# Placing: POOL makes the second one-hots of three batches in four

## The reference, cut to what matters

```python
q = (x @ w_q).reshape(N, PEER_HEADS, 2, PEER_D_HALF)
s = jnp.einsum('nhpd,pkd->nhpk', q, sub_keys)            # 8 heads, 2 halves, 128 keys each
s_top, i_top = lax.top_k(s, PEER_TOPK)                   # 16 of each half
cand = (s_top[:, :, 0, :, None] + s_top[:, :, 1, None, :]).reshape(N, PEER_HEADS, 256)
best, best_pos = lax.top_k(cand, PEER_TOPK)              # 16 pairs
expert = idx1 * N_KEYS + idx2                            # one of 128 x 128 experts
g = softmax(best)
act = gelu(einsum('cd,ced->ce', x_c, u[e_c]))            # 128 experts per token
out = einsum('ce,ced->cd', g_c * act, v[e_c])
```

## Time and profile before

| | |
|---|---|
| runs | 3749.11 us median (3741.89 to 3754.56, 3 runs) |
| profiled execution | 3739.43 us, span 3737.3 us |
| mean granted clock of TensorE | 0.927 |
| busy share of the span | PE 84%, DVE 71%, ACT 28%, POOL 53% |
| placing | from about 1565 to 1787.5 us, its loop about 216 us |

### The profile page before, as it was taken

One profiled execution on the slowest core, in us unless ns is written; L12 is line 12 of the kernel. 1 busy time (PEld: TensorE's weight loads), 2 busy tenths in 40 slices (PEclk: granted clock), 3 DMA queues, 4 the chain that ended last, 5 costly groups with the idle time before them and its releaser, 6 DMA issues. The chain is left out here.

```text
span 3737.3 us, 47455 instructions
## 1 busy us (share of the span) xinstructions
PE 3150.9 (84%) x15281; PEld 2082.0 (56%) x15281; DVE 2641.1 (71%) x5953; ACT 1045.5 (28%) x1817; POOL 1983.8 (53%) x1776
## 2 busy tenths in 40 slices
PE   5687699789859989377477899998999999999995
PEld 4446244556424333266355667676666666766663
DVE  2226788698475687999677778787777787886446
ACT  4441044366111000276311222222222222222112
POOL 0001565454245887222367677776777677776443
PEclk9888899899979999688788999999999999999997
DMA  6523577766577997258899999999999999999996
GB/s 244 201 85 120 170 265 248 215 214 215 221 251 284 314 339 246 102 172 245 315 379 374 353 408 408 404 405 382 409 399 408 381 405 404 408 405 378 366 345 240
DMA packets 411751, 1133.01 MB, mean 303 GB/s; under 512 B 34088, under 2 KB 129576, under 8 KB 411488
## 3 DMA queue, kind: packets, MB, share of 16 engines
q0 software_dynamic: 221184, 805.40, 57.7%
q1 hardware_dynamic: 174544, 317.82, 23.5%
q10 hardware_dynamic: 15888, 8.13, 0.7%
HBM read 1077.51 MB, written 53.71 MB: 303 GB/s over the span
## 5 line engine op out<-in xcount | busy, mean ns | idle before, releaser
L2272 POOL DMA_INDIRECT exp_value_row<-in_v_rows,exp_v_id x568 | 715.2, 1259 | 278.2 <-issue 176.1
L2319 DVE CUSTOM_DVE_ANT_0 edge_row<-edge_row,edge_x 128x1024 f32<-128x1024 f32 x480 | 583.6, 1218 | 289.0 <-DMA edge_row<-in_u_rows,edge_u_id 255.0
L2264 POOL DMA_INDIRECT edge_row<-in_u_rows,edge_u_id x480 | 508.2, 1059 | 329.2 <-DVE edge_dot L2319 178.3
L376 POOL DMA_INDIRECT ahead_row<-in_u_rows,keep_expert_id x256 | 336.3, 1314 | 347.8 <-DVE keep_dot L386 284.6
L2153 PE MATMUL exp_a_ps<-exp_xT_hi,exp_u_hi 128*128 128x512 f32 x1024 | 409.7, 400 | 19.1 <-DVE exp_u_lo L2288 10.0
L2168 PE MATMUL exp_o_ps<-exp_v_hi,exp_w_hi 128*128 128x512 f32 x1024 | 339.1, 413 | 80.5 <-DVE keep_acc L2383 80.3
L2153 PE MATMUL exp_a_ps<-exp_xT_lo,exp_u_hi 128*128 128x512 f32 x1024 | 401.5, 392 | 0.0
L2153 PE MATMUL exp_a_ps<-exp_xT_hi,exp_u_lo 128*128 128x512 f32 x1024 | 401.1, 392 | 0.0
L2383 DVE TENSOR_TENSOR keep_acc<-exp_o_ps,keep_acc 128x1024 f32<-128x1024 f32 x256 | 311.5, 1219 | 115.9 <-PE exp_o_ps L2168 114.6
L386 DVE CUSTOM_DVE_ANT_0 ahead_row<-ahead_row,ahead_x 128x1024 f32<-128x1024 f32 x256 | 304.0, 1220 | 76.6 <-DMA ahead_row<-in_u_rows,keep_expert_id 72.9
L2139 PE MATMUL exp_v_ps<-exp_value_row,exp_hot 128*32 128x512 f32 x2272 | 278.6, 602 | 60.5 <-DMA exp_value_row<-in_v_rows,exp_v_id 60.1
(11 more groups left out here) (380 smaller groups left out, 5134.3 us busy)
## 6 DMA issues: line engine op xcount, KB each, us to landing
edge_u_raw<-in_uT SPq DMA_DIRECT2D x130, 512.0 KB, 6.7
exp_v_raw<-in_v_rows SPq DMA_DIRECT2D x128, 512.0 KB, 6.7
exp_g_raw<-scratch_g SPq DMA_DIRECT2D x128, 256.0 KB, 8.3
scratch_g<-place_grid SPq DMA_DIRECT2D x3, 8192.0 KB, 36.2
proj_ctx_mod_slab<-in_w_mod SPq DMA_DIRECT2D x8, 2048.0 KB, 14.4
cheads_room<-in_w_in SPq DMA_DIRECT2D x10, 1024.0 KB, 5.1
heads_early_room<-in_w_in SPq DMA_DIRECT2D x10, 1024.0 KB, 9.7
exp_value_row<-in_v_rows,exp_v_id POOLq DMA_INDIRECT x568, 7.7
```

Of the source, the lines that this page charges most:

```text
L376: nc.gpsimd.indirect_dma_start(out=ahead.row[:, n % KEY_RING, :], out_offset=None, in_=io["u_rows"], in_offset=bass.IndirectOffsetOnAxis(a ...
L2264: nc.gpsimd.indirect_dma_start(out=key_row[:, j % RING, :], out_offset=None, in_=io["u_rows"], in_offset=bass.IndirectOffsetOnAxis(ap=u_id ...
L2272: nc.gpsimd.indirect_dma_start(out=value_row[:, 4 * (j % 2) + t, :], out_offset=None, in_=io["v_rows"].rearrange("a b n -> (a b) n"), in_o ...
L2319: nc.vector.tensor_tensor_reduce(out=key_row[:, j % RING, :], in0=key_row[:, j % RING, :], in1=x, scale=1.0, scalar=0.0, op0=ALU.mult, op1 ...
```

## The change

A third table, `SECOND_BY_POOL`, names batches 0, 1 and 2. Their second one-hots are made by POOL, in four operations of 128 columns, one token each, comparing `iota` with one number per partition. DVE's comparison of batches 0 and 2 now covers the first keys only (512 columns), batch 1 keeps its four scaled comparisons, and batch 3 stays as it was. PE waits in addition for `second_ready` in those batches. POOL's queue changes order: four gathers first, then a wait for `cols`, then per step twelve comparisons and, up to step 27, the gather that lies four ahead.

```diff
--- before.py
+++ after.py
@@ -1789,7 +1789,7 @@
     first, second, weight = routes
     UNITS = PEER_HEADS // 2 * LATENT_TILES
     BATCH, BATCHES = 4, 4
-    SCALED_BY_ACT, SCALED_BY_DVE = (0, 2), (1, 3)
+    SCALED_BY_ACT, SCALED_BY_DVE, SECOND_BY_POOL = (0, 2), (1, 3), (0, 1, 2)
     STEP = BATCH * BATCHES
     STEPS = P // STEP
     PER_TILE = STEPS * BATCHES
@@ -1808,6 +1808,7 @@
         hot_ready = s.sem("hot_ready")
         scaled = s.sem("scaled")
         dve_ready = s.sem("dve_ready")
+        second_ready = s.sem("second_ready")
         made = s.sem("made")
         placed = s.sem("placed")
         stored = [s.sem(f"stored{n}") for n in range(2)]
@@ -1819,10 +1820,32 @@
                 for m in range(STEPS):
                     body(t, m, t * STEPS + m)
 
+        def second_keys(engine, t, m, b):
+
+            at = m * STEP + b * BATCH
+            if engine is nc.gpsimd:
+                for k in range(BATCH):
+                    last = nc.gpsimd.tensor_scalar(hot[:, b, 1, k, :], keep["iota"][:, :], cols[:, t, 1, at + k:at + k + 1],
+                                                   None, ALU.is_equal)
+                return last
+            return engine.tensor_tensor(
+                hot[:, b, 1, :, :], keep["iota"][:, :].unsqueeze(1).broadcast_to([P, BATCH, N_KEYS]),
+                cols[:, t, 1, at:at + BATCH].unsqueeze(2).broadcast_to([P, BATCH, N_KEYS]), ALU.is_equal)
+
         @block.gpsimd
         def _(pool):
-            for n in KEYS:
+            for n in KEYS[0:KEY_RING]:
                 gather_keys(nc, io, ahead, pool, n)
+            pool.wait_ge(cols_ready, DENSE_TILES)
+
+            def body(t, m, before):
+                for b in SECOND_BY_POOL:
+                    if before:
+                        pool.wait_ge(made, BATCHES * (before - 1) + b + 1)
+                    second_keys(nc.gpsimd, t, m, b).then_inc(second_ready, 1)
+                for n in KEYS[KEY_RING + before:KEY_RING + before + 1]:
+                    gather_keys(nc, io, ahead, pool, n)
+            walk(body)
 
         @block.vector
         def _(dve):
@@ -1845,14 +1868,12 @@
                         dve.wait_ge(made, BATCHES * (before - 1) + b + 1)
                     if b in SCALED_BY_ACT:
                         nc.vector.tensor_tensor(
-                            hot[:, b, :, :, :],
-                            keep["iota"][:, :].unsqueeze(1).unsqueeze(1).broadcast_to([P, 2, BATCH, N_KEYS]),
-                            cols[:, t, 0:2, at:at + BATCH].unsqueeze(3).broadcast_to([P, 2, BATCH, N_KEYS]),
+                            hot[:, b, 0, :, :], keep["iota"][:, :].unsqueeze(1).broadcast_to([P, BATCH, N_KEYS]),
+                            cols[:, t, 0, at:at + BATCH].unsqueeze(2).broadcast_to([P, BATCH, N_KEYS]),
                             ALU.is_equal).then_inc(hot_ready, 1)
                     else:
-                        nc.vector.tensor_tensor(
-                            hot[:, b, 1, :, :], keep["iota"][:, :].unsqueeze(1).broadcast_to([P, BATCH, N_KEYS]),
-                            cols[:, t, 1, at:at + BATCH].unsqueeze(2).broadcast_to([P, BATCH, N_KEYS]), ALU.is_equal)
+                        if b not in SECOND_BY_POOL:
+                            second_keys(nc.vector, t, m, b)
                         for k in range(BATCH):
                             last = nc.vector.tensor_scalar(
                                 hot[:, b, 0, k, :], keep["iota"][:, :], cols[:, t, 0, at + k:at + k + 1],
@@ -1878,6 +1899,8 @@
                         pe.wait_ge(scaled, 2 * before + SCALED_BY_ACT.index(b) + 1)
                     else:
                         pe.wait_ge(dve_ready, 2 * before + SCALED_BY_DVE.index(b) + 1)
+                    if b in SECOND_BY_POOL:
+                        pe.wait_ge(second_ready, len(SECOND_BY_POOL) * before + SECOND_BY_POOL.index(b) + 1)
                     if before:
                         pe.wait_ge(placed, BATCHES * (before - 1) + b + 1)
                     for k in range(BATCH):
```

## The result

The changed kernel takes 3850.02 us (median of 4 runs, 3845.75 to 3856.07); the kernel before, beside it on the same chip, 3747.90 (3741.89 to 3754.56). The ratio is 1.0281, 95% interval 1.0261 to 1.0302: 102 us slower. The forecast was 17 us slower, and its range ended at 3814. The sign was right, the size and the range were not.

What follows compares the result with a forecast made beforehand. DVE was taken to bound placing at 6.75 us a step; a step of 7.17, 0.50 above 6.67, adds 16 us over 32 steps, plus 1 at the start: 3739.4 + 16 + 1 = 3756 profiled, 3766 median; range 3737 to 3814.

Steps and rivals of the forecast that it cites:

- The price of the comparison: In placing, P, POOL's time for one 128-column comparison, was put at 0.30 us, between 0.23 and 0.41.
- The exclusion: In placing, POOL's twelve comparisons a step don't run beside DVE's work but are added; each exchange overlaps 0.18 us.
- 12 P + 5.01 - 8 x 0.18: Placing's step time: twelve POOL comparisons plus DVE's 5.01, less eight exchanges' overlap; 7.17 us with P = 0.30.
- 3.57: In placing's step sum, the part beside 12 P: DVE's 5.01 less 8 x 0.18, in us.
- DVE alone needs 5.01: In placing, the change takes 1.66 us a step off DVE's 6.67, so DVE alone would need 5.01.
- The floor of 5.6: Least placing step for ACT and PE: ACT's 4.67 us plus 0.96 for PE's last batch.
- The ring: In placing, ACT and PE waiting on each other: ACT's last copy waits for PE's last batch; floor 5.6 us a step.
- my first rival: In placing, exclusion does not bite on short operations; 5.6 us a step decides, 35 us less, 3715; chance 12%.
- the second: Rival in placing: POOL's comparison costs 0.23, the scalar is free; 6.33 us a step, 11 us less, 3739; chance 14%.
- 0.20: Chance given to a faster kernel: the first rival and some half of the second.
- What the next profile would show: In placing's loop: POOL above 75% busy, comparisons around 0.35 us with tail to 1.4, no dot waits, PE waiting for POOL.
- The start, the gathers, the stores: Placing's first product starts 0.7 us later, counted as 1 us; moved gathers and shifted stores cost nothing.

Runs made afterwards that it cites:

- e_price: Kernel before plus series of POOL operations ahead of placing, first alone, then beside DVE's 512-wide and scaled comparisons; its one run took 3790.86 us.
- e_prod: Changed kernel with POOL multiplying iota by iota in place of each comparison, second keys of batches 0 to 2 left out; ratio 1.0102 to the kernel before.
- e_left_order: Changed kernel, POOL's second keys made in the first step only, ACT scaling the next step's batch 0 before copying batch 3; ratio 0.9855 to the kernel before.
- e_left: Changed kernel with POOL making second keys in the first step only, left out in all later ones; ratio 1.0018 to the kernel before.
- e_fill: Changed kernel with POOL memsets in place of its comparisons, second keys of batches 0 to 2 left out; ratio 1.0004 to the kernel before.
- e_order: Kernel before with only ACT's order changed: it scales the next step's batch 0 before copying batch 3; ratio 0.9981 to the kernel before.

## Why the prediction was wrong

- **The price of the comparison.** "The cast, with one input and the same 128 columns, is the nearest row", P = 0.30 with 0.41 as the upper end: this step failed. It measured 0.58. In the forecast's own sum that is 0.28 x 12 x 32 = 107 us more, on top of the 17 forecast, of which the next step takes back 0.35 x 32 = 11. Both ends were taken from operations of another form. The Trainium skill (GPSIMD Engine Reference, "Performance pitfalls for Q7 kernels") has each small read command cost about 102 cycles; no run here shows such a cost for the scalar, as with and without one from SBUF a comparison takes 0.58 and 0.59.
- **The exclusion.** "They are added to it", 12 P + 5.01 - 8 x 0.18, was wrong in its mechanism and nearly right in its number. With P = 0.58 it gives 10.53, measured 10.18. But DVE's step isn't in the sum; POOL's is: comparisons 6.96, gather 1.24, and 2 us sat out behind DVE's dot and its 512-wide operations, with DVE idle for 43% of the loop. That 3.57 and 1.24 + 2.0 lie close together is luck. The rows I had the earlier trace rows were of long POOL products, which do hold DVE up; e_price shows short comparisons held up by DVE instead, 0.7 us against 0.09. The same account holds for the product (e_prod), not for the copies.
- **DVE alone needs 5.01.** Right: 5.00 in e_left_order.
- **The floor of 5.6.** Right for a step at 2.4 GHz (5.69), and wrong for the loop, because I took PE's 3.84 from one step at the full clock although gave a granted clock of 0.83. The ring took 6.77 in the stretch shown and 6.83 in e_left, so my first rival's 3715 could not have come true: with POOL's work for nothing (e_left) the time is that of before. Nor could the second's 3739 as a gain by 11 us. With POOL's work free or nearly so (e_left, e_fill) nothing was gained, so no lower price of the comparison would have made this change clearly faster; 0.20 was too much for that side.
- **What the next profile would show.** Right: POOL above 75% of the loop (97%), no waits for dots, PE behind POOL, DVE idle for PE, and a long tail of comparisons that sat out a dot (up to 1.64). Wrong: comparisons "around 0.35". Two of the signs of being wrong are there: a spacing other than 0.30, for the price, and DVE's operations at 0.69 and 1.21 in the median, for the exclusion.
- **The start, the gathers, the stores.** The first product comes at 1575.1 us, 3.5 later than the 1571.6 of before, not 0.7: POOL's first two comparisons, beside DVE's 512-wide ones, start 1.18 and 0.84 us before the next, not 0.30. Those 3.5 us and 31 steps of 3.43 make up the loop's 109.5, so stores and gathers cost next to nothing in it; DVE waited for a gathered row once, 0.5 us. The profiled executions differ by 106.6 us over the whole span, the medians by 102, which is within what single executions differ by.

## What to carry to other kernels

Before work is moved off the busiest engine, build (or work out) the version in which that work is simply gone: it gives the next bound, and here it would have shown that nothing was to be won until ACT's scaling left PE's ring. A second bound within two per cent of the first doesn't show in busy shares or in the waits of the busiest engine; it shows where another engine waits once in every step for a third, and in its start-to-start times over several steps, with its clock. And a price on an engine is taken only from an operation of the same form; where there is none, the range has to reach well beyond the neighbours.

## What was not expected of the hardware

- On POOL an operation of a tensor with a scalar costs about 0.26 us and 2.2 to 2.7 ns a column (e_price; 128 columns: 0.58), dearer than the product of two tensors (0.36) and than a copy (0.24); a comparison costs the same as a multiplication.
- Beside DVE's 512-wide comparisons POOL's take 1.30 us each and cost DVE 0.09 in two operations; beside DVE's scaled comparisons of 128 columns they keep their 0.58 and cost DVE 0.06 each (e_price). Twelve back-to-back copies on POOL hold one scaled comparison of DVE for over 2 us. Which side starves depends on the kind of operation, in a way that these runs don't settle; memsets on POOL held DVE up nowhere that showed in the step (e_fill).
- TensorE's clock took part in the ring. In e_left PE idles 1.85 us before each step's batches, and in 22 of 31 steps the clock then falls to 1.2 GHz for some of them; in e_left_order it idles 1.17 us, and stays at 2.4. The step fell by 6.83 - 5.00 = 1.8 us for 0.7 us of that wait. But the wait ahead of the step doesn't decide it: in e_order PE idles as long there, and 0.71 us once more in the middle, and is at the full clock in 27 of 31 steps.

```profile
1649.62 2.05 PE L1884 MATMUL place_ps<-place_hot 128*128 128x128 f32 x16 [1.86 <-ACT place_hot L1897]
1652.38 2.05 PE L1884 MATMUL place_ps<-place_hot 128*128 128x128 f32 x16 [0.71 <-ACT place_hot L1897]
```

By what rule the clock is granted isn't shown.
